# Routing and the first block of a two-block transformer kernel: held router weights, a table by matrix products, and chains of small work issued earlier

## What is computed

```python
mod = silu(c) @ w_ada + b_ada                       # six vectors of 1024: sh1, sc1, g1, sh2, sc2, g2
h = rms_norm(x, norm1_g) * (1 + sc1) + sh1
q, k, v, gu, gv, ga, gb = split(h @ w_in)
y_a = sliding_window_attention(q, k, v, positions, sinks, rel_bias)     # blocks of 128, bias by distance
y_b = gelu(gu) * (w_s @ layer_norm(gelu(gv)) + b_s)                     # spatial gating
merged = sigmoid(ga) * (y_a @ p_a) + sigmoid(gb) * (y_b @ p_b)
x = x + g1 * (merged @ w_o)
h = rms_norm(x, norm2_g) * (1 + sc2) + sh2
# routing: logits of 4 groups and 32 experts, best group, best 2 experts in it, weights by exp,
# rank of each (token, choice) among those of its expert, a table of blocks of 128 rows for each expert
x = x + g2 * experts(h[table rows])                 # 32 experts, each 6 units of 1 MB of weights
```

## Time and profile before

| | |
|---|---|
| median of 3 runs | 3284.31 us (3283.97 to 3289.2) |
| the profiled execution, its own time | 3289.22 us |
| its span, first to last instruction | 3287.5 us |
| mean granted clock of PE | 0.937 of 2.4 GHz |
| first product with `whi` | 76.75 us |
| last product of `wo1` ends | 524.64 us |
| transposes of the first gathered rows | 610.81 us |
| experts, after that | to about 1210 us |

### The profile page before, as it was taken

How to read it: one execution, slowest core, us unless ns; L and a number is a source line. 1 busy time by engine, 2 the same in 40 slices (tenths; PEclk the granted TensorE clock), 3 DMA queues, 4 the chain that set the end, 5 groups by cost and what they waited for, 6 DMA issues and landing times.

```text
span 3287.5 us, 37251 instructions
## 1 busy us (share of the span) xinstructions
PE 2884.8 (88%) x13585; PEld 2396.6 (73%) x13585; DVE 2274.0 (69%) x3002; ACT 1503.7 (46%) x2000; POOL 599.3 (18%) x520
## 2 busy tenths in 40 slices
PE   2767897599999967999999899999988779999996
PEld 1445676488888855777777678999988778788884
DVE  5544553588888864397965317989887767888885
ACT  2224422488788843344443223564455533333332
POOL 1120010211111110000000000001125443444441
PEclk6879898799999978999999899999998889999998
DMA  6443344499999951333334334566678899999993
GB/s 250 140 139 130 133 141 118 150 371 371 366 358 359 358 202 60 110 103 103 102 110 147 112 109 146 185 230 234 216 267 316 316 358 340 359 373 364 370 361 104
DMA packets 199901, 746.51 MB, mean 227 GB/s; under 512 B 25264, under 2 KB 74720, under 8 KB 142368
## 3 DMA queue, kind: packets, MB, share of 16 engines
q1 hardware_dynamic: 118960, 490.83, 41.5%
q0 software_dynamic: 59744, 188.13, 16.4%
q10 hardware_dynamic: 21008, 65.09, 5.2%
HBM read 670.90 MB, written 98.20 MB: 234 GB/s over the span
## 4 chain that ended last, share of the span: by engine, by line
PE 54%; DVE 16%; DMA 8%; issue 7%; ACT 4%; POOL 1%; ACTq 0%; DVEq 0%; POOLq 0%
PE PS L508 46%; DVE wlo L1708 4%; DMA gbuf<-in_peer_u_dram,IDX 3%; DVE oh L2394 2%; DVE hf L2408 1%; ACT whi L1113 1%; DVE hf L2420 1%; PE PS L925 1%; PE PS L937 1%; ACT HH L1679 1%; DMA ht<-in_peer_u_dram,IDX 1%; DMA sN<-s_scratch 1%; PE PS L773 1%; PE PS L554 1%; DMA sq<-in_peer_u_dram,IDX 1%
## 5 line engine op out<-in xcount | busy, mean ns | idle before, releaser
L1708 DVE TENSOR_TENSOR wlo<-raw,whi 128x2048 fp32r<-128x2048 f32 x392 | 894.3, 2289 | 389.2 <-ACT whi L1113 336.4
L1113 ACT ACTIVATE whi<-raw 128x2048 fp32r<-128x2048 f32 x392 | 751.0, 1917 | 368.9 <-PE PS L508 312.0
L508 PE MATMUL PS<-HH,whi 128*128 128x512 f32 (+1 forms) x2056 | 797.9, 388 | 55.2 <-DVE HL L1759 31.5
L508 PE MATMUL PS<-HL,whi 128*128 128x512 f32 (+1 forms) x2056 | 760.5, 370 | 0.0
L508 PE MATMUL PS<-HH,wlo 128*128 128x512 f32 (+1 forms) x2056 | 759.4, 369 | 0.0
L508 PEld LDWEIGHTS PS<-HH,whi 128*128 128x128 f32 x2056 | 397.9, 194 | 116.4 <-issue 47.5
L508 PEld LDWEIGHTS PS<-HL,whi 128*128 128x128 f32 x2056 | 398.1, 194 | 46.5 <-issue 7.0
L508 PEld LDWEIGHTS PS<-HH,wlo 128*128 128x128 f32 x2056 | 396.8, 193 | 44.2
L508 PE MATMUL PS<-whi,HH 128*128 128x512 f32 (+1 forms) x896 | 351.8, 393 | 49.4 <-DVE wlo L1708 31.0
L508 PE MATMUL PS<-whi,HL 128*128 128x512 f32 (+1 forms) x896 | 347.0, 387 | 0.0
L508 PE MATMUL PS<-wlo,HH 128*128 128x512 f32 (+1 forms) x896 | 346.9, 387 | 0.0
(11 more groups left out here) (406 smaller groups left out, 3962.9 us busy)
## 6 DMA issues: line engine op xcount, KB each, us to landing
raw<-in_moe_dram SPq DMA_DIRECT2D x192, 1024.0 KB, 7.5
raw<-in_u_units_dram SPq DMA_DIRECT2D x64, 1024.0 KB
raw<-in_v_units_dram SPq DMA_DIRECT2D x64, 1024.0 KB
raw<-in_w_in_dram SPq DMA_DIRECT2D x44, 1024.0 KB
raw<-in_w_ada_dram SPq DMA_DIRECT2D x24, 1024.0 KB
acts_dram<-sS ACTq DMA_DIRECT2D x64, 384.0 KB
gates_dram<-XT ACTq DMA_DIRECT2D x24, 1024.0 KB
sS<-acts_dram SPq DMA_DIRECT2D x42, 384.0 KB, 7.5
```

The source lines that it names most:

```text
L508: ins = t.matmul(dst, a, b, start=(first and n == 0), stop=(last and n == 2))
L1113: a.inc(a.e.activation(m.whi[p % HRING][:, :, :], m.raw[RAW_SLOT[load_of(p)]][:, :, :], ACT.Copy), "hi", p)
L1708: v.inc(v.e.tensor_tensor(m.wlo[h][:, :, :], m.raw[RAW_SLOT[load_of(p)]][:, :, :], m.whi[h][:, :, :].bitcast(F32), ALU.subtract), "lo_v", p)
```

## The change

In words, by stage:

- Start. Loads 0 to 7 go to 8 different buffers. Of the first 8 units of `w_ada` DVE now takes 4 (the even ones); PE multiplies the odd ones with `c` itself, 16 products of 128x1 with `raw` as weights and 4 with `acc` in each of 4 groups. The preparation of the bias work, and its first mask, come first on DVE; the reciprocal and the first two `ht` come after its second unit. `hf`, `HH` and `HL` of neighbouring chunks are interleaved. The 4 MB fill waits for the fifth unit (`ada` 4).
- Bias. One comparison of `prow` with `prow + thr` gives `mask`, which has two buffers, and step 1's mask comes at the first tick. The second fill comes after step 2, and the first two `bt` after step 3; `bt` lies in `sq` and `ht`.
- Local work. The layer norm is spread over the softmax steps, with one root for all four. Sigmoid(x) is made from Tanh(x/2), with +1 in the gating operations and a factor 0.5 in `mod`. The inputs of pa are split within gb1, half of those of wo within pb1.
- Route. The sums of the squares begin within wo1. The router's weights `wr` are held and `H2` moves: 8 products of 512 columns, the bias added on ACT, 4 transposes. Both exponentials are ahead of most of the row copies. `Ms`, the triangle and the ones are bf16. The table is made on chip: comparisons give `blk` and `slot`, 8 products sum `put` into PSUM, three small DVE operations write `TB`. The 8 scatters, the read back and the cleared table are gone; `xg` is cleared early.

The core of the diff:

```diff
@@ raw_slots
-    ring, last, slots, before, fresh = deque(range(RING)), {}, [], [], {}
+    ring, last, slots, before, fresh = deque(range(RING + MORE)), {}, [], [], {}
+        if n == RING + MORE:
+            ring = deque(range(RING))
@@ pe_modulation
-    pe.wait_ge("ada", 2 * nb + 1)
+    if nb < 4:
+        pe.wait_ge(raw_sem(load), load)
+        raw = m.raw[RAW_SLOT[load]]
+        pe.wait_ge("ada", 2 * nb)
...
+        if nb < 4:
+            for c in range(4):
+                t.matmul(dst, raw[:, c, 128 * j:128 * j + 128], m.col("c")[:, 4 + c:5 + c], start=(c == 0), stop=False)
@@ pe_first, wo1 (and a sum of squares after each step of its second unit)
+    tick = pe_late_squares(pe, m)
@@ pe_route
-    for i in range(NT):
-        for kc in range(KC):
-            ins = t.matmul(m.PS[:, 0, 36 * i:36 * i + 36], m.H2[:, kc, 128 * i:128 * i + 128], m.wr[:, kc, :],
+    for kc in range(KC):
+        ins = t.matmul(m.PS[0:36, 0, :], m.wr[:, kc, :], m.H2[:, kc, :], start=(kc == 0), stop=(kc == KC - 1))
+    for i in range(NT):
+        ins = t.transpose(m.PS[:, 1, 256 + 36 * i:292 + 36 * i], m.lgT[:, 128 * i:128 * i + 128], m.ident[0:36, 0:36])
...
+    for n in range(8):
+        ins = t.matmul(m.PS[:, 2, 0:3 * N_BLK], R["slot"][:, n, :], R["put"][:, n, :, :].rearrange("p c b -> p (c b)"),
+    pe.inc(ins, "listed")
@@ act_local, act_first
+        if n == 3:
+            a.wait_ge("bnst", 3)
+            a.inc(s.activation(m.sd4[:, :], m.mv[:, :, 1], ACT.Sqrt, bias=m.epst[:, 0:1]), "sdev")
...
-                a.inc(s.activation(m.hf[:, k % 2, :], m.PS[:, j, :], ACT.Sigmoid), "ev", f"{w}{n}", j)
+                a.inc(s.activation(m.hf[:, k % 2, :], m.PS[:, j, :], ACT.Tanh, scale=0.5), "ev", f"{w}{n}", j)
@@ dve_local: at the second step of each pair n; the sixth call waits for the root
+        next(norm, None)
+        next(norm, None)
@@ dve_route
-    step(e.scalar_tensor_tensor(out=dst[:, :, :], in0=tm2[:, :, :], scalar=128.0, in1=dst[:, :, :],
-    step(e.tensor_copy(m.dsti[:, :, :], dst[:, :, :]), "placed")
+    v.inc(e.tensor_tensor(R["blk"][:, :, :], ..., ALU.is_equal), "route")         # 128 x 312
+    v.inc(e.tensor_tensor(R["slot"][:, :, :], ..., ALU.is_equal), "route")        # 128 x 1024
+    v.inc(e.tensor_tensor(R["put"][:, :, :, :], ..., ALU.mult), "placed")         # 128 x 936
@@ pool_route
-            g.dma(e.indirect_dma_start(m.tab[:, :], bass.IndirectOffsetOnAxis(ap=m.dsti[:, k, i:i + 1], axis=0),
-    g.dma(e.dma_start(m.TB[:, :, :], m.tab[:, :].rearrange("(b p) c -> p b c", p=128)), "table_in")
+    g.wait_ge("tabled")
```

More of the change, by code:

```diff
@@ L422, in __init__ @@
             self.oraw = self.raw[RING:RING + 2]
+        rows.close()
         with ExitStack() as st:
@@ L669, in drain, with pe_late_squares, tick @@
         pass
+def pe_late_squares(pe, m):
+    k = -4
+    def tick(p, j):
+        nonlocal k
+        if k >= 0:
+            if k == 0:
+                pe.wait_ge("gate_a", 3)
+            pe.wait_ge("sq", 1, k)
+            pe.inc(pe.e.matmul(m.PS[:, 7, :], m.ones[:, :], m.sq[:, k % 2, :], start=(k == 0), stop=(k == KC - 1)),
+                   "ssq", 1, k)
+        k += 1
+    return tick
 def pe_first(pe, m):
@@ L1186, in act_local @@
         yield
-    for i in range(NT):
-        a.wait_ge("bnst", i)
-        a.inc(s.activation(m.sd4[:, i:i + 1], m.mv[:, i, 1:2], ACT.Sqrt, bias=m.epst[:, 0:1]), "sdev", i)
-        yield
-    yield
     for g in range(4):
@@ L1259, in act_first, with first_squares @@
     act_project(a, m, "wo0", places("w_o", 0, 2), None)
-    act_project(a, m, "wo1", places("w_o", 2, 2), None)
-    a.mark("first_done")
+    kc = 0
+    def first_squares():
+        nonlocal kc
+        if kc < 2:
+            a.wait_ge("evv", "wo0", kc)
+            a.inc(s.activation(m.sq[:, kc, :], m.XT[:, kc, :], ACT.Square), "sq", 1, kc)
+        kc += 1
+    act_project(a, m, "wo1", places("w_o", 2, 2), None, first_squares)
+    a.mark("first_done")
+    for kc in range(2, KC):
+        a.wait_ge("evv", f"wo{kc // 4}", kc % 4)
+        a.wait_ge("ssq", 1, kc - 2)
+        a.inc(s.activation(m.sq[:, kc % 2, :], m.XT[:, kc, :], ACT.Square), "sq", 1, kc)
+    a.wait_ge("ssq", 1, KC - 1)
+    a.wait_ge("nx", 0, KC - 1)
+    a.inc(s.activation(m.rstd[:, :], m.PS[:, 7, :], ACT.Sqrt, bias=m.epst[:, 0:1], scale=1.0 / D), "rstd", 1)
     a.wait_all("first_done")
@@ L1272, in act_route @@
                            bias=m.mod[:, 24 + kc:25 + kc]), "ha", 1, kc)
+    a.wait_ge("logit", 0)
+    a.wait_ge("w_r")
+    a.inc(s.activation(m.lgT[:, :], m.PS[0:36, 0, :], ACT.Identity, bias=m.br[:, 0:1]), "lgt")
+    a.wait_ge("gdiff")
+    a.inc(s.activation(R["gx"][:, :, :], R["gx"][:, :, :], ACT.Exp), "gexp")
     for i in range(NT):
+        if i == 1:
+            a.wait_ge("ediff")
+            a.inc(s.activation(R["dd"][:, :], R["dd"][:, :], ACT.Exp), "eexp")
         for half in range(2):
@@ L1794, in dve_local @@
     e = v.e
+    norm = dve_gate_norm(v, m)
     for n in range(9):
@@ L1869, in dve_first, with normed @@
     e = v.e
-    for i in range(8):
-        dve_modulation(v, m, i)
+    side = dve_bias(v, m)
+    next(side)
+    def normed(kc):
+        if kc > 1:
+            v.wait_ge("ha", 0, kc - 2)
+        v.inc(e.tensor_tensor(m.ht[:, kc % 2, :], m.XT[:, kc, :], m.rstd[:, :], ALU.mult), "nx", 0, kc)
+    for nb in range(4):
+        dve_modulation(v, m, 2 * nb)
+        if nb == 1:
+            dve_inverse(v, m, 0)
+            normed(0)
+            normed(1)
     v.wait_ge("modp", 3)
@@ L2552, in pool_first @@
     bias(7)
-    for k in range(4, 16):
+    for k in range(4, 14):
         gate(k)
```

330 lines of the change are left out of this document (183 added, 147 removed), and 1 row of the table n.

## The result

The changed kernel takes 3188.09 us (median; 3184.83 to 3191.53) against 3285.75 us before in the same session (3283.97 to 3289.2): a ratio of 0.9702, interval 0.9685 to 0.9718. The forecast was 3174 with a range of 3145 to 3201. The profiled execution took 3187.84 us, at the median of its runs; its span is 3186.1 us, 101.4 less than before.

The account below looks back on a forecast made before the run. PE was taken to set the first block's pace, through its waits and the half rate after them. Terms 3.5 - 40 - 34 - 4 - 36.2 = -110.7 took 3289.2 to 3178.5, less 4.9 for the median: 3174 us, range 3145 to 3201.

Parts of the forecast that it names:

- pa to wo: Stage before the route: splitting wo's inputs early shortens the 5.6 us wait before wo; -4 us, bounds -1 and -8.
- Start: Up to the first product: one-column products on PE at half rate make it 3.5 us longer, bounds -11 to +7.
- Rival (1): Start: PE's one-column products run at full rate, 14 us go, 3160 us in all; chance 0.2.
- Bias: Bias stage: PE's waits for `mask` and half rate behind them go; -40 us, bounds -30 and -44.
- The mask term: Bias stage: 37.0 us of PE's waits for `mask` plus 2.2 us half rate behind three of them, 43.6 us.
- rival (2): Stalls return elsewhere and half of the bias and local terms is lost, +37 us, 3211 us; chance 0.16.
- Local: Local stage: bias tile 16.0, layer norm 11.7, tables 10.0, less 3.6 for a new wait; -34 us, bounds -24 and -44.
- The root: Local stage: layer norm at pair 2 waits for the root ACT issues at pair 3, PE's products 3.6 us later.
- The gates' tables: Local stage: fewer Sigmoid and Exp table loads shorten four pairs' waits for `Pt`, 10.0 us with half rate.
- Route: Route stage: squares, logits, exponential, ranks, placing and table together give -36.2 us, bounds -28 and -40.
- The ranks: Route: bf16 takes one record a product, 3.1 us instead of 6.2; -3.0 us, bounds 0 and -5.
- the squares: Route: three sums move into wo1's stream (+2.6 us), one step is left after it; -4.2 us with this.

Follow-up runs that it names:

- a2: Changed kernel with DVE's bias preparation and first mask behind the modulation's four units instead of in front: 3174.79 us.
- a3: Changed kernel with two bev buffers instead of one, so ACT's copies wait for the store of the step before last: 3173.12 us.
- b1: Changed kernel with preparation behind the modulation, first w_in unit split ahead of mod, two bev buffers, root at pair 2 and four gate buffers: 3150.76 us.
- b3: The kernel with all five edits together, its start reordered and the last of PE's four units on DVE: 3139.83 us, ratio 0.9547 to before.
- c0: The changed kernel run again without edits, to see how far a stage repeats: 3186.15 us.
- a5: Changed kernel with two parts undone, gates by Sigmoid again and ranks in fp32 again: 3200.45 us.

## Why the prediction was right, and where it was not

The order of the steps and the sign of each term but one (pa to wo) held, and the time lies in the range, 14 us above the forecast. The stages fall short of the forecast by 9.3 us together, and 17 us of shortfall (start, bias, pa to wo) stand against 8 us of gains that weren't forecast (local, route, rest), so the sum is better than its terms. The terms for `mask`, the bias tile, the layer norm, the logits, the exponential and the table weren't undone one by one; that their waits went is read from the lists and timelines above. By its steps:

**Start, +3.5 said, +6.9 measured.** Half rate was right, and the group of 20 took 8.55 us instead of 9.3. I had divided the length of a row of four products (1.86 us) by four; but rows overlap: in the changed kernel such a row is 1.84 us long, and the next one begins 1.71 us behind its start, 0.43 us a product. Wrong was "I let DVE begin the first unit at 20 us": DVE waited for `thr` until 18.57, then did the preparation and also the first mask (2.3 us), which I had not counted ahead of the units, and began the first unit at 25.3 us; PE began at 28.3 instead of 23. a2 shows that this order cost 12.3 us: PE began 8.4 us later (28.3 for 19.9), and it lost the one group that it could have done at full rate (4.0 us). Rival (1), full rate, is refuted: PE busy for 34 us without a gap stayed at 0.50. The rule of the Trainium skill behind it (TensorE: Matmul & The Clock Gate, Part 1) does not hold for these products: the window from 45 to 55 us has 10.00 us busy of 10.00 at 0.50, and a2's window from 25 us on the same behind a stretch at 1.00. The Trainium skill also has a load paid by its columns (TensorE: Matmul & The Clock Gate, Part 2). That agrees in kind: the weight loads, 128 columns for one column of data, are busy for 10.00 of these 10.00 us too. In size it agrees at full rate only: an estimate by its formula is 0.107 us a load, and a product with its two loads took 0.22 us at full rate, but 0.43 us here.

**Bias, -40 said, -30.9 measured.** The mask term was right in mechanism and size: with a3 the stage is 43.2 us shorter than before, against 43.6 counted. The step that fell short is "Going on in this way through gv, k, v and q I find no later mask that PE would wait for". It held for the mask (0.5 us), but I had followed only `mask`, not the other resource of the same loop. With the mask in time a step follows the one before so closely that the single `bev` buffer is not yet stored. Removing it gave 9 to 12 us. It is rival (2), stalls that return, in one place of the stage only.

**Local, -34 said, -37.5 measured.** The root cost 2.4 to 3.7 us (3.6 said), through DVE's chain as described, though in b1 and b3, with other edits around it, the same move shortened the stage by 0.2 and 1.6 us only. The gates' tables were worth 14.1 to 15.4 us, not 10.0: I had counted the waits of four pairs that held a load and one stretch of half rate for them all, but each longer wait has its own. The Trainium skill (ScalarE: Activation LUTs, What ACT_TABLE_LOAD costs) makes a switch 2.66 us, and an estimate by it makes the term 18. The rows have 1.28 us for each load here too, and where ACT had been busy just before (the root's load at 232.36 begins 0.03 us behind the activation before it) nothing was added; that the stage lost more than my 10 is the clock, not the load. For the bias tile and the norm 27 us remain (37.5 - 14.1 + 3.7; by c0 it is 38.8 - 15.4 + 2.4 = 25.8), against 27.7 said; they weren't tried one by one.

**pa to wo, -4 said, +0.6 measured** without the sums of squares (-1.0 in c0). The early splitting works only as far as the gates come back, and "about 1.5 us stay" was too little: PE waited 5.5 us, and the clock fell behind it. With four buffers the term is -9.

**Route, -36.2 said, -37.6 measured.** Logits 8.3 us (9.3 said) and the exponential (7.6 us less) are as worked out. The ranks came 5.7 us shorter instead of 3.0, and not by bf16 alone: a5's 3.3 us in fp32 show that half of the gain is the clock, since the products now follow row transposes at full rate. I had carried the half rate of the old place, 0.22 us a record, to the new one. The table's eight products took 3.76 us (3.6 said), at clock 0.50, and from `put` to the gather it was 5.3 us (4.6 said). That the sum is near is in part luck: against the ranks stand the squares, -2.1 us instead of -4.2. I had one sum left behind wo1's last product; there were five, and the logits began 12.0 us behind wo1's end (before: 16.7), with 2.6 us paid inside it.

**The end.** I took 4.9 us off because the profile of before lay above its median; that of the changed kernel lies at its own. Such a correction belongs in the range. The rest of the program was 3 us shorter, which is what it varies by (2667 to 2677 us over all runs).

**Its own signs.** The start at clock 0.50, the waits for `mask` and the first bias tile, and the root's wait (9.95 us on DVE, 3.5 on PE) came as said, and of the twelve table loads the trace has eleven (of the 26 before it has 25). One sign of being wrong was met as well: the local stage's waits of PE are 14.5 + 3.5 + 2.2 = 20.2 us, above the 20 given (c0: 20.0). By the prediction's own terms they should have been 19.2 (46.7 before, less 13.8, 9.5 and 7.8, plus 3.6), so that limit left no room; the stage was shorter than said because the waits that went took more half rate with them than counted. The experts, from their first transposes to the last product's start, took 588.8 us (before: 589.3), under the 596 given.

## What to carry to other kernels

When a stall is removed, follow every resource of the loop that now runs faster (buffers on their way to DRAM above all), not only the one that was late; a second buffer on idle partitions cost nothing here and gave 9 to 12 us. Price each wait of TensorE with the half rate that follows it: for Pt and the gates the waits (6.7 and 6.4 us) were a half and two thirds of what their removal gave. And before work is given to an idle engine, ask what it costs there: at the start a unit in one-column products took TensorE 6.8 us where VectorE takes 3, and of the two cuts run in the same order (four units on TensorE, or two: first product at 71.4 and 66.2 us) the better was the one at which both engines ended together. And run such gains together before adding them up: in b1 the root's wait went, but the stage's clock was lower, and one gain of five didn't show.

## What the runs showed of the hardware

- TensorE busy without a gap with fp32 products of one column stays at the lower level (0.50) for 34 us, and falls to it from 1.00 while busy (a2). It takes 0.43 us a product there and 0.22 at the upper level, and in the window from 45 to 55 us the weight loads are busy for 10.00 of 10.00 us: the time of such a product is that of its loads of 128 columns.
- 14 bf16 products of 32 columns with 128-column weights took 0.5 us, the same in fp32 3.3 us at the same clock (two records each): not two, but over six times as long.
- A store of 64 KB to DRAM landed in 3.2 us (median), but in up to 7.9 us in the bias stage, where the 1 MB loads run; in the kernel before it was 2.9 us, and 3.5 at most.
- Of two executions of one kernel, the bias stage was 100.1 and 103.4 us, with the same waits of PE (8.9 and 8.5 us for `bev`): the clock, 0.97 and 0.93, made the difference.
